# The sparse stage starts with the index projection instead of the queries, and the small set-up is turned in one run

## What is computed

```
h = rms_norm_2(x, g_pre_mix[l])
proj = h @ w_in[l]
u_pool, q, k, v, iq, ik, iw = jnp.split(proj, SPLIT_POINTS, axis=-1)   # 512 512 512 512 512 64 8
q, k, iq, ik = (each with rope_partial at `positions`)
iw = iw * (IDX_HEADS ** -0.5)
a_out = pool_mixer(u_pool, w_pool[l], pool_scale[l])
b_out = dsa_attention(q, k, v, iq, ik, iw, topk)
mix = jnp.concatenate([a_out, b_out], axis=-1) @ w_out[l]
x = x + rms_norm_2(mix, g_post_mix[l])
```

```
logits = jnp.einsum('bqhd,bsd->bqhs', iqb, ik32) * (IDX_DIM ** -0.5)
score = jnp.einsum('bqh,bqhs->bqs', iwb, jax.nn.relu(logits))
top_val, top_idx = lax.top_k(score, topk)            # 64 keys for each query
# softmax attention of q to the chosen keys and values
```

## Time and profile before

| | us |
|---|---|
| median of 3 runs | 2010.02 (2008.75 to 2016.38) |
| profiled execution | 2010.11 |
| its span | 2008.3 |
| TensorE busy | 1898.4 (95%) |
| VectorE busy | 1255.1 (62%) |
| ScalarE busy | 1040.7 (52%) |
| GpSimd busy | 200.9 (10%) |

### The profile page before, as it was taken

How to read it: one execution, slowest core, us unless ns; L and a number is a source line. 1 busy time by engine, 2 the same in 40 slices (tenths; PEclk the granted TensorE clock), 3 DMA queues, 4 the chain that set the end, 5 groups by cost and what they waited for, 6 DMA issues and landing times.

```text
span 2008.3 us, 28132 instructions
## 1 busy us (share of the span) xinstructions
PE 1898.4 (95%) x11049; PEld 1648.6 (82%) x11049; DVE 1255.1 (62%) x1646; ACT 1040.7 (52%) x1505; POOL 200.9 (10%) x247
## 2 busy tenths in 40 slices
PE   7999998999999999999899999999889999979998
PEld 6788897878888888889787888887678888767887
DVE  5666656665766676665675576666766556666555
ACT  5555544545555565554454555555455555554553
POOL 1010101010000001010110000002000111200110
PEclk9999998999999999999999999999999999989999
DMA  8586643344565467656334346556225554524552
GB/s 289 181 270 189 181 157 102 101 146 163 169 199 190 155 224 251 214 150 204 106 106 157 124 160 203 191 174 219 88 88 188 190 196 147 203 85 137 191 188 82
DMA packets 232086, 339.49 MB, mean 169 GB/s; under 512 B 22343, under 2 KB 182225, under 8 KB 231953
## 3 DMA queue, kind: packets, MB, share of 16 engines
q1 hardware_dynamic: 224048, 307.91, 47.0%
q0 software_dynamic: 7904, 29.78, 4.4%
HBM read 336.62 MB, written 1.05 MB: 168 GB/s over the span
## 4 chain that ended last, share of the span: by engine, by line
PE 81%; DVE 11%; ACT 4%; issue 1%; POOL 1%; DMA 1%; DVEq 0%; SPq 0%; POOLq 0%; ACTq 0%
PE ps L1569 79%; ACT region L656 3%; PE ps L1574 2%; DVE wlo L1051 2%; DVE xn L1051 1%; DVE xn L1059 1%; DVE region L1059 1%; DVE ahl L1051 1%; DVE mlo L1051 1%; ACT ahl L656 1%; DVE sm L1067 1%; DVE xs L1059 1%; DMA raw<-ffn_w_gate 1%; DVE region L1494 0%; DVE sm L1055 0%
## 5 line engine op out<-in xcount | busy, mean ns | idle before, releaser
L1051 DVE TENSOR_TENSOR wlo<-raw,whi 128x1024 fp32r<-128x1024 f32 (+2 forms) x462 | 564.0, 1221 | 265.0 <-ACT whi L656 230.9
L656 ACT ACTIVATE whi<-raw 128x1024 fp32r<-128x1024 f32 (+2 forms) x462 | 484.3, 1048 | 48.0 <-PE ps L1569 12.4
L1569 PE MATMUL ps<-ahl,whi 128*128 128x512 f32 (+1 forms) x2048 | 462.6, 353 | 2.8 <-DVE region L1051 2.8
L656 ACT ACTIVATE region<-ps 128x512 f32<-128x512 f32 (+3 forms) x312 | 180.5, 579 | 492.9 <-PE ps L1569 435.3
L1569 PEld LDWEIGHTS ps<-ahl,whi 128*128 128x128 f32 x2048 | 354.0, 190 | 49.0 <-DVE region L1051 3.2
L1569 PE MATMUL ps<-whi,ahl 128*128 128x512 f32 (+2 forms) x1104 | 303.0, 355 | 22.8 <-DVE ahl L1059 10.4
L1569 PE MATMUL ps<-ahl,wlo 128*128 128x256 f32 x1680 | 287.0, 282 | 0.0
L1569 PEld LDWEIGHTS ps<-ahl,wlo 128*128 128x128 f32 x1680 | 249.5, 191 | 12.8
L1569 PEld LDWEIGHTS ps<-whi,ahl 128*128 128x128 f32 x1104 | 199.4, 195 | 56.3 <-DVE ahl L1051 15.8
L1569 PE MATMUL ps<-wlo,ahl 128*128 128x512 f32 (+2 forms) x552 | 192.8, 349 | 0.0
L1051 DVE TENSOR_TENSOR mlo<-raw,mhi 128x1024 fp32r<-128x1024 f32 (+1 forms) x130 | 158.3, 1218 | 37.5 <-ACT mhi L656 27.1
(11 more groups left out here) (154 smaller groups left out, 2333.5 us busy)
## 6 DMA issues: line engine op xcount, KB each, us to landing
raw<-w_ff SPq DMA_DIRECT2D x64, 1024.0 KB, 5.2
raw<-ffn_w_gate SPq DMA_DIRECT2D x44, 1024.0 KB, 5.5
raw<-ffn_w_up SPq DMA_DIRECT2D x44, 1024.0 KB, 5.7
raw<-ffn_w_down SPq DMA_DIRECT2D x44, 1024.0 KB, 5.0
raw<-w_in SPq DMA_DIRECT2D x38, 1024.0 KB, 5.9
raw<-w_out SPq DMA_DIRECT2D x16, 1024.0 KB, 4.9
raw<-xa_wk SPq DMA_DIRECT2D x8, 1024.0 KB, 5.1
raw<-xa_wv SPq DMA_DIRECT2D x8, 1024.0 KB, 5.2
```

Source lines behind the costliest of these rows:

```text
L656: e.activation(o, i, f, **kw).then_inc(*act.did(*names))
L1051: e.tensor_tensor(o, a, b, op).then_inc(*dve.did(*names))
L1569: m = e.matmul(o, l, r, start=start, stop=stop)
```

## The change

The items iq and ik (two each, 292 columns by 4 k steps) become three items `index` of 584 columns with 3, 3 and 2 k steps, and they come first. The stage's first product is theirs: each k step makes three products of 292 columns into bank m and three into bank 4 + m. The items of q (512 columns) follow as a block into banks 2 and 3; k, v and u go to banks 0 and 1. The rest of the stage is written in a new order: transposes of the index part ahead of k, q's transposes behind `index(1)`, v and u in between, and u's second half behind the first values. `first_items(s)[-2:]` places the turn's splits by the last two of the three items. In the set-up the cast of the positions moves to the end of the third tile, and TensorE's three turns stand together.

```diff
             wi = A["w_in_2"][l, :, :]
-            for tag, c0, n in (("q", 512, 512), ("iq", 2048, 292), ("ik", 2340, 292), ("k", 1024, 512), ("v", 1536, 512),
-                               ("u", 0, 512)):
+            for k0, k1 in ((0, 3), (3, 6), (6, 8)):
+                item(s, "index", rows(wi, k0, k1, 2048, 2632), k1 - k0, 584)
+            for tag, c0, n in (("q", 512, 512), ("k", 1024, 512), ("v", 1536, 512), ("u", 0, 512)):
...
-                 "memory": (("wq", 0), ("wq", 1)), "sparse": (("q", 0), ("q", 1))}
+                 "memory": (("wq", 0), ("wq", 1)), "sparse": (("index", 0), ("index", 1), ("index", 2))}
...
-                i0, i1 = first_items(s)
+                i0, i1 = first_items(s)[-2:]
                 split_to(i0 + 1)
...
(scalar, sparse)
                 for m in range(2):
                     q.wait_ge(*pe.at("first", s, m))
-                    put(qn[:, m * 512:(m + 1) * 512], PS[:, m, :], ACT.Copy, ("q", l) if m else ("q", l, 0))
+                    put(iqk[:, m, 0:292], PS[:, m, 0:292], ACT.Copy, ("iq_first", l, m))
+                    put(iqk[:, m, 292:576], PS[:, 4 + m, 0:284], ACT.Copy, ("iq_rest", l, m))
+                for m in range(2):
+                    put(iw[:, m, :], PS[:, 4 + m, 284:292], ACT.Copy, ("iq", l) if m else ("iw", l), scale=8.0 ** -0.5)
                 for c in range(2):
-                    take(s, "iq", c)
-                q.wait_ge(*pe.at("iq", l))
-                for m in range(2):
-                    put(iqk[:, m, 0:292], PS[:, 2 + m, 0:292], ACT.Copy, ("iq_first", l, m))
...
+                    take(s, "q", c)
+                natural((2, 3), qn, "q")
+                heads(iqT, 4, "iqT")
                 for c in range(2):
                     take(s, "k", c)
-                heads(iqT, 5, "iqT")
-                natural((2, 3), kn, "k")
                 index(0)
                 take(s, "v", 0)
+                natural((0, 1), kn, "k")
                 index(1)
+                q.wait_ge(*dve.at("score", l, 0))
+                heads(sqT, 2, "sqT")
                 take(s, "v", 1)
+                heads(skT, 2, "skT")
                 take(s, "u", 0)
-                natural((2, 3), V, "v")
-                q.wait_ge(*dve.at("score", l, 0))
-                heads(sqT, 0, "sqT")
-                heads(skT, 2, "skT")
-                take(s, "u", 1)
+                natural((0, 1), V, "v")
                 exps("s", l, 0, 128, sP, 1.0)
                 exps("s", l, 1, 128, sP, 1.0)
-                natural((0, 1), U, "u")
                 turned(0)
                 turned(1)
+                take(s, "u", 1)
+                natural((0, 1), U, "u")
...
(vector, set-up)
+            def positions():
+                q.wait_ge(*const_in["pos"].at("in"))
+                cp(pos_row, pos_in, ("pos_row",))
...
-                q.wait_ge(*pe.at("pet"))
+                q.wait_ge(*pe.at("pos"))
                 cp(SM[:, 0:72], PS[:, 2, 0:72], ("pet",))
-                q.wait_ge(*const_in["pos"].at("in"))
-                cp(pos_row, pos_in, ("pos_row",))
-                q.wait_ge(*pe.at("pos"))
                 cp(posf, PS[:, 2, 128:130], ("posf",))
...
+                        if s == 0 and j == 2:
+                            positions()
...
(vector, sparse)
                 score(0)
+                take(s, "v", 0)
+                select(0)
+                score(1)
                 take(s, "v", 1)
-                select(0)
-                take(s, "u", 0)
-                score(1)
                 head(0)
-                take(s, "u", 1)
                 head(1)
                 select(1)
+                head(2)
                 out(0)
                 out(1)
-                head(2)
+                take(s, "u", 0)
+                take(s, "u", 1)
...
(tensor, product)
-                        o = PS[:, m, 0:w] if by_k else PS[:, m, i * 256:(i + 1) * 256]
+                        nk, w = hi.shape[1:3]
+                        if w == 584:
+                            outs = [(PS[:, m, 0:292], slice(0, 292)), (PS[:, 4 + m, 0:292], slice(292, 584))]
+                        else:
+                            outs = [(PS[:, m, 0:w] if by_k else PS[:, m, i * 256:(i + 1) * 256], slice(0, w))]
                         for kk in range(nk):
-                            if (i == 1 and kk >= nk - nk // 4) != (part == 1):
+                            if (i == last and kk >= nk - max(1, nk // 4)) != (part == 1):
                                 continue
...
(tensor, sparse)
-                natural(s, "iq", (2, 3), 292, ("iq", l))
-                q.wait_ge(*act.at("q", l))
-                natural(s, "ik", (0, 1), 292, ("ik", l))
-                q.wait_ge(*act.at("iq_first", l, 1))
-                natural_part(s, "k", 0, (2, 3), 512)
+                natural(s, "q", (2, 3), 512, ("q", l))
                 q.wait_ge(*pool.at("ik_rope", l))
+                q.wait_ge(*act.at("iq", l))
                 for m in range(2):
-                    turned(PS[:, 4, m * 128:(m + 1) * 128], iqk[:, m, 512:640], 128, *([("ikT", l)] if m else []))
-                heads(iqk, 5, "iqT")
-                natural_part(s, "k", 1, (2, 3), 512, ("k", l))
+                    turned(PS[:, 6, m * 128:(m + 1) * 128], iqk[:, m, 512:640], 128, *([("ikT", l)] if m else []))
+                heads(iqk, 4, "iqT")
+                natural_part(s, "k", 0, (0, 1), 512)
                 index(0)
-                q.wait_ge(*act.at("k", l))
-                natural_part(s, "v", 0, (2, 3), 512)
+                natural_part(s, "k", 1, (0, 1), 512, ("k", l))
                 index(1)
-                natural_part(s, "v", 1, (2, 3), 512, ("v", l))
                 q.wait_ge(*pool.at("q_rope", l))
-                q.wait_ge(*act.at("iq", l))
-                heads(qn.rearrange("p (m n) -> p m n", m=2), 0, "sqT")
+                heads(qn.rearrange("p (m n) -> p m n", m=2), 2, "sqT")
+                q.wait_ge(*act.at("k", l))
+                natural_part(s, "v", 0, (0, 1), 512)
                 q.wait_ge(*pool.at("k_rope", l))
-                q.wait_ge(*act.at("v", l))
+                q.wait_ge(*act.at("sqT", l, 1))
                 heads(kn.rearrange("p (m n) -> p m n", m=2), 2, "skT")
-                q.wait_ge(*act.at("sqT", l, 1))
-                natural_part(s, "u", 0, (0, 1), 512)
+                natural_part(s, "v", 1, (0, 1), 512, ("v", l))
                 q.wait_ge(*act.at("index", l, 1))
                 q.wait_ge(*act.at("skT", l, 1))
                 scores(0)
                 scores(1)
-                natural_part(s, "u", 1, (0, 1), 512, ("u", l))
+                q.wait_ge(*act.at("v", l))
+                natural_part(s, "u", 0, (0, 1), 512)
                 turn_scores(0)
                 turn_scores(1)
                 q.wait_ge(*dve.at("s_shift", l, 1, 1))
                 scores(2)
+                values(0)
+                values(1)
+                natural_part(s, "u", 1, (0, 1), 512, ("u", l))
                 q.wait_ge(*act.at("u", l))
                 scores(3)
-                values(0)
-                values(1)
```

More of the change, by code:

```diff
@@ L1469, in sparse @@
                 l = STAGES[s][1]
-                for tag in ("iq", "ik"):
-                    for c in range(2):
-                        take(s, tag, c)
+                for c in range(2):
+                    take(s, "q", c)
+                q.wait_ge(*pe.at("ikT", l))
+                cp(ikT, PS[:, 6, 0:256], ("ikT", l))
                 for c in range(2):
                     take(s, "k", c)
-                q.wait_ge(*pe.at("ikT", l))
-                cp(ikT, PS[:, 4, 0:256], ("ikT", l))
-                take(s, "v", 0)
                 def score(m):
@@ L1601, in product @@
                 def product(m, part):
+                    last, k0 = len(it) - 1, 0
                     for i, n in enumerate(it):
                         hi, lo = weights(n)
[L1604 to L1606 removed]
+                        nk, w = hi.shape[1:3]
[3 more added lines that the diff above has]
+                            outs = [(PS[:, m, 0:w] if by_k else PS[:, m, i * 256:(i + 1) * 256], slice(0, w))]
                         for kk in range(nk):
[L1608 removed]
+                            if (i == last and kk >= nk - max(1, nk // 4)) != (part == 1):
                                 continue
[L1610 removed]
+                            k = k0 + kk if by_k else kk
                             q.wait_ge(*dve.at("a", s, m, k // 4))
                             ms = slice(m * 128, (m + 1) * 128)
[L1613 to L1617 removed]
+                            for o, c in outs:
+                                names = []
+                                if kk == nk - 1 and c.stop == w:
+                                    names = [("used", n)] if m else []
+                                    names += [("first", s, m)] if i == last else []
+                                three(o, ahv[:, k, ms], alv[:, k, ms], hi[:, kk, c], lo[:, kk, c], k == 0, k == 7, *names)
```

(3 more changed lines are left out.)

19 lines of the change are left out of this document (2 added, 17 removed).

## The result

| | before | after |
|---|---|---|
| median of 4 runs, us | 2009.41 (2008.75 to 2016.38) | 1982.95 (1982.11 to 1984.59) |
| span of the profiled execution, us | 2008.3 | 1980.6 |
| mean granted clock | 0.982 | 0.988 |

The account below looks back on a forecast made before the run. TensorE, 81% of the chain of waits, was taken to bound the kernel, losing idle time and then slow clock. First stage -11.7, second -10.3, set-up -6.2: -28.2 from 2010.1 gives 1982 us, range 1976 to 1989 (chance 0.66).

Parts of the forecast that it names:

- Set-up, -6.2: Set-up: moving the positions' cast removes TensorE's 3.93 us wait and 2.25 us of slow clock behind it, -6.2 us.
- The turn, second half's product 1.65 and 0.95 later: Turns into the sparse stages: splitting a third item delays this product; net +0.65 us in the first, -0.05 in the second.
- Idle time: Each sparse stage: 9.4 us of TensorE waits go (6.1 ScalarE, 2.8 GpSimd's copy, 0.5 others).
- Slow clock: Sparse stages: products at 1.2 GHz behind waits return to full clock, 4.05 us in the first, 1.55 in the second.
- New waits, 1.55 and 0.4: Each sparse stage: TensorE newly waits 1.55 us for u's evictions before the scores, and 0.4 for v's.
- The tie on the fourth item: Sparse stage: q's second half is split by 1388.7, TensorE wants it at 1389.0; cost 0, at worst 0.5 us.
- The wait before the first output product, 4.2 with its clock loss: Sparse stages: some 4.2 us of wait for VectorE stays, clock loss unchanged; up to -4.4 us in all if that doesn't come.
- Some 3 us of slack: Selection in each sparse stage: VectorE can be some 3 us late before TensorE waits.
- the VectorE rival: Sparse stages: VectorE 8 us later than forecast, 5 us of wait return per stage; 1993 us, chance 0.20.
- The rotation's slack, 2.9: First sparse stage: GpSimd's index rotation ends at 1391.6, TensorE gets there at 1394.5, 2.9 us of slack.
- The starved rotation: Rival: VectorE's splits hold back GpSimd's last four rotation steps, TensorE waits 2.4 us per sparse stage; 1987 us, chance 0.06.
- The two-bank product: Rival: index products writing two banks lose overlap, 0.48 us each instead of 0.136, +66 us; 2048 us, chance 0.04.

Follow-up runs that it names:

- set-up alone: Kernel before with only the positions' cast moved behind the third tile and TensorE's three turns put together: 2006.44 us, 0.9969 of before.
- nine more maxima: Changed kernel with nine more Max8 reads on VectorE ahead of the first selection in each sparse stage: 1992.27 us, 0.9896 of before.
- 30 products: Changed kernel with 30 small identity products in the wait before each sparse stage's first output product: 1984.93 us, 0.9866 of before.
- 19: Changed kernel with third item's differences in VectorE's turn gaps, second values behind u's second half, 19 small products in the last wait: 1975.80 us, 0.9830 of before.
- Twelve more steps: Changed kernel with twelve more 144-element GpSimd steps ahead of the index rotation in each sparse stage: 1998.74 us, 0.9946 of before.

## Why the prediction was right, step by step

- *Set-up, -6.2.* Right in both parts: no wait, 24 products in 83.55 - 77.97 = 5.6 us as forecast (7.8 before). In its place it gave 6.4, alone and in the change. What I didn't ask is whether all of it arrives: 2.2 us went again in the third slow stretch near 1000 us. By ratio the set-up alone is worth 3.8 to 8.4 us.
- *The turn, second half's product 1.65 and 0.95 later.* Six products of the first half's rest, then it begins: 1371.93 - 1358.93 = 13.0 behind the turn's start against 1375.20 - 1364.64 = 10.56. That is 2.4, with 0.7 of slow clock in it, so 1.7. In the second stage 1680.16 - 1667.09 against 1695.78 - 1683.47: 0.8, since the turn's first wait fell from 2.05 to 1.31 as the narrower differences had it (forecast 0.7).
- *Idle time.* From the turn's start to the first output product, the turn's first wait included, TensorE's gaps sum to 16.1 us before and 8.5 after in the first stage, 17.1 and 9.3 in the second: 7.6 and 7.9 less. The terms forecast -9.4 - 0.84 + 1.95 + 0.65 = -7.6 and -9.4 - 1.25 + 1.95 - 0.05 = -8.8.
- *Slow clock.* The first stage lost the 4.05 us as forecast, and 1.7 came new behind the turn's wait of 1.74; with 1.0 us that no term covers, this makes the difference between 11.7 and 10.95. I had put such falls into the range, behind the 1.55 us waits, and not into the turn, where I made a wait longer.
- *The second stage gave 1.2 more than forecast.* The clock term there was too small: it held the 1.55 us of one stretch and missed the stretch of 3.4 us in the turn (1686.90), which cost 1.7. So 3.25 us of clock went instead of 1.55, and 0.9 us less of idle time than forecast. With 7.9 and 3.25, 0.4 us of the 11.5 remain unassigned, and 1.0 in the first stage.
- *New waits, 1.55 and 0.4.* 1.32 and 0.22. The tie on the fourth item came out without a wait.
- *The wait before the first output product, 4.2 with its clock loss.* 4.25, down from 4.99 and 5.41, so the terms of 0.84 and 1.25 came as 0.74 and 1.16; and 5.5 us for twelve products in place of 3.0 in both stages.
- *"Some 3 us of slack" on VectorE in the selection* was too much: 1.4. Nothing hung on it here, but the VectorE rival starts 1.6 us earlier than I priced it, and it can cost more than its waits: in the run with nine more maxima one stage paid 7.2 us for 1.5 us of wait, the other 1.15.
- *The rotation's slack, 2.9.* 2.64. The starved rotation didn't come: its two late steps took 2.80 as before.
- *The cast costs 0.9 if its gap were gone.* It costs 0.2 there. The 0.93 was mostly a wait for GpSimd's step, which that profile had too.
- *Rivals.* The two-bank product runs at (1367.00 - 1361.56) / 40 = 0.136 us per product: nothing serialised. Set-up alone was 2006, not 2004, and is not what happened.
- *How close the number came is in part luck.* The mechanism is right: the waits that were to go went, those that were to come came. But the misses of the three parts (0.5 and 0.75 us too much, 1.2 too little) cancel, and the profiled execution of the change reached the first sparse product at 1361.56, the earliest of the twelve kernels with the new set-up (up to 1365.65). This scatter alone is larger than the 1 us between 1982 and 1982.95.

## What to carry to other kernels

Ask of a stage's first product who waits for its result longest: put first the one with the longest chain on the slow engines behind it, and give TensorE the blocks that nobody waits for to do meanwhile. Load an engine on purpose with a few harmless instructions to measure a slack; it is cheap. The slack forecast for VectorE from the kernel before was off by a factor of two (3 us against 1.4), while the 1.2 read from the new kernel's own trace was close. A wait is paid twice where the clock falls behind it, and work put into the wait must be cut to its length: 30 products gave 0.8 us of tail and nothing in the time, 19 gave 2.0 us per stage.

## What the runs showed of the hardware

- VectorE's small instructions stand still beside a GpSimd step, by their operands. VectorE in the kernel after, in order of time:

```profile
80.59 0.43 DVE L1058 COPY sm<-ps 128x72 f32<-128x72 f32 x2
81.06 0.80 DVE L1046 TENSOR_TENSOR sm<-sm,small 128x16 f32<-128x16 f32 x1
```

GpSimd beside it:

```profile
80.53 1.30 POOL L510 TENSOR_TENSOR hlo<-region,hhi 128x512 fp32r<-128x512 f32 x1 [14.75 <-ACT hhi L657]
```

The two copies out of PSUM run through (0.2 each) while GpSimd is busy; the sum of two inputs from SBUF, 0.18 before, ends at 81.86, just after GpSimd at 81.83. The cast from SBUF to SBUF did the same above. The Trainium skill (SBUF — State Buffer, "Who interferes with whom") says that a VectorE instruction with two SBUF inputs, and a cast in its two-port mode, share a port pair with GpSimd, and that who issues first holds it for the whole instruction. By that rule both should end with GpSimd's step and the PSUM copies pass: the trace agrees in all three. That the cast ran in its two-port mode is not shown by any view; only its end is.
- The other way round, GpSimd's 144-element steps took 0.49 us with VectorE idle and 1.35 beside its differences, and the copy 0.29 (VectorE idle) or 1.17. Twelve more steps made the first sixteen 14.18 us long: six of them beside VectorE's differences at 1.35, the other ten at 0.49. Beside such a row of differences GpSimd got one step in per VectorE instruction, which took 1.33 us instead of 1.25, and was never held out for the row.
- The clock fell behind a wait of 1.74 us in the first stage's turn and not behind one of 1.72 in the second's. This is not scatter alone: in the eight profiled kernels with these two waits (1.70 to 1.74 us) it fell in the first stage each time, and in the second once. Why, no run shows. Behind the 4.25 us waits it fell each time, for 3.4 or 6.8 us, and in the second stage each of the six stretches of 3.4 us was followed by another some 34 us later. This is worth 1 to 2 us per place, and limits what a single edit's trace can tell.
